# Samples' values in four column groups with a fold at the end, and a new order in the loop of a layer-1 attention kernel

## The reference, cut to what matters

```python
def _nsa_block(qg, gates, q_pos, cmp_k, cmp_v, ksb, vsb, kw, vw, kw_pos):
    s = jnp.einsum('bqghd,bngd->bghqn', qg, cmp_k).astype(jnp.float32) * scale
    p = jax.nn.softmax(jnp.where(cmask, s, NEG_INF), axis=-1) * cmask
    o_cmp = jnp.einsum('bghqn,bngd->bqghd', p.astype(cmp_v.dtype), cmp_v)
    ...
    ps = jax.nn.softmax(jnp.where(smask, ss, NEG_INF), axis=-1)
    o_sel = jnp.einsum('bghqk,bgqkd->bqghd', ps.astype(vsel.dtype), vsel)
    ...
    pw = jax.nn.softmax(jnp.where(wmask, sw, NEG_INF), axis=-1)
    o_win = jnp.einsum('bghqk,bkgd->bqghd', pw.astype(vw.dtype), vw)
    return gates[..., 0:1] * o_cmp + gates[..., 1:2] * o_sel + gates[..., 2:3] * o_win
```

## Time and profile before

| | us |
|---|---|
| median of 3 runs | 977.55 (976.17 to 978.6) |
| the profiled execution | 977.28 |
| its span, first to last instruction | 975.6 |
| attention loop with the samples' keys, window looked at | 684 to 800 |
| the samples' softmax | 800 to 836 |
| the samples' values | 836 to 912 |
| output projection | 912.38 to the end |

### The profile page before, as it was taken

One profiled execution on the slowest core, in us unless ns is written; L12 is line 12 of the kernel. 1 busy time (PEld: TensorE's weight loads), 2 busy tenths in 40 slices (PEclk: granted clock), 3 DMA queues, 4 the chain that ended last, 5 costly groups with the idle time before them and its releaser, 6 DMA issues.

```text
span 975.6 us, 15843 instructions
## 1 busy us (share of the span) xinstructions
PE 921.6 (94%) x5202; PEld 497.5 (51%) x5202; DVE 475.1 (49%) x965; ACT 293.3 (30%) x716; POOL 232.2 (24%) x321
## 2 busy tenths in 40 slices
PE   6999999999899999999999999998888888899998
PEld 3544444444455543454565766566444444556444
DVE  1157778779345552122234172715667776556211
ACT  5101111103454550032101111425555565445100
POOL 0000223210033330430424242001334443234000
PEclk9999999999999999999999999998999998999999
DMA  9142665593254567772414232020211231131211
GB/s 352 57 167 101 226 233 177 193 287 80 45 155 148 156 220 256 220 179 92 143 34 144 73 99 84 16 80 12 65 50 54 74 103 69 48 92 57 89 44 44
DMA packets 86070, 117.59 MB, mean 121 GB/s; under 512 B 21006, under 2 KB 49886, under 8 KB 85678
## 3 DMA queue, kind: packets, MB, share of 16 engines
q1 hardware_dynamic: 66432, 80.96, 25.7%
q0 software_dynamic: 9920, 27.31, 9.5%
q10 hardware_dynamic: 9648, 8.41, 2.7%
HBM read 108.68 MB, written 11.36 MB: 123 GB/s over the span
## 4 chain that ended last, share of the span: by engine, by line
PE 87%; DVE 5%; DMA 3%; ACT 3%; issue 1%; SPq 1%; ACTq 0%; DVEq 0%
PE ps L719 26%; PE ps L976 11%; PE ps L982 6%; PE ps L1269 6%; PE ps L999 4%; PE ps L728 3%; PE ps L1150 3%; PE ps L1161 3%; PE ps L1038 3%; PE ps L914 3%; PE ps L1226 2%; DMA arena<-cache_sb_v 2%; PE ps L892 2%; PE ps L864 1%; PE ps L1016 1%
## 5 line engine op out<-in xcount | busy, mean ns | idle before, releaser
L719 PE MATMUL ps<-wring,arena 128*128 128x512 f32 x448 | 198.4, 602 | 1.5 <-issue 1.5
L719 PEld LDWEIGHTS ps<-wring,arena 128*128 128x128 f32 x448 | 85.2, 192 | 105.8 <-issue 105.7
L667 POOL TENSOR_TENSOR z<-z,work 128x1024 f32<-128x1024 f32 (+1 forms) x64 | 80.2, 1253 | 200.5 <-DVE work L1983 199.7
L976 PE MATMUL ps<-wring,z 128*128 128x512 f32 (+2 forms) x320 | 108.4, 494 | 0.0
L1501 ACT ACTIVATE z<-ps,work 128x512 f32<-128x512 f32 (+3 forms) x128 | 66.6, 527 | 70.3 <-DVE work L1975 58.4
L1324 ACT ACTIVATE z<-ps 128x512 f32<-128x512 f32 (+1 forms) x64 | 27.4, 433 | 181.8 <-PE ps L719 147.5
L976 PEld LDWEIGHTS ps<-wring,z 128*128 128x128 f32 x320 | 55.4, 192 | 44.5 <-issue 42.9
L358 POOL DMA_DIRECT2D arena<-cache_sb_k x64 | 34.4, 537 | 167.4 <-DVE work L1618 143.1
L1823 DVE TENSOR_TENSOR arena<-ps,consts 128x512 f32<-128x512 f32 x32 | 30.4, 1024 | 83.9 <-PE ps L1016 83.9
L1512 ACT ACTIVATE arena<-ps 128x512 f32<-128x512 f32 (+3 forms) x128 | 48.9, 438 | 31.6 <-PE ps L1150 31.6
L1975 DVE TENSOR_REDUCE work<-ps 128x1 f32<-128x512 f32 (+3 forms) x128 | 56.9, 486 | 2.2
(11 more groups left out here) (317 smaller groups left out, 1271.0 us busy)
## 6 DMA issues: line engine op xcount, KB each, us to landing
wring<-w_in SPq DMA_DIRECT2D x12, 2048.0 KB, 9.7
arena<-cache_sb_k POOLq DMA_DIRECT2D x64, 256.0 KB, 3.0
arena<-cache_sb_v SPq DMA_DIRECT2D x64, 256.0 KB, 3.5
wring<-w_out SPq DMA_DIRECT2D x3, 2048.0 KB, 7.8
arena<-cache_sel_k SPq DMA_DIRECT2D x64, 64.0 KB, 1.8
consts<-cache_sel_v SPq DMA_DIRECT2D x64, 64.0 KB, 1.8
consts<-aux SPq DMA_DIRECT2D x1, 2299.5 KB, 16.3
xres<-x_prompt SPq DMA_DIRECT2D x4, 512.0 KB, 10.2
```

The lines of the kernel that those rows point to most:

```text
L667: nc.gpsimd.tensor_tensor(P_u(n), P_u(n), bc(coef(n).unsqueeze(2), [P, 2, (NT - n % NT) * P]), ALU.mult).then_inc(n_scaled, 1)
L719: mm = pe.matmul(ps[:, t, 0:width], stat, mov, start=(k == 0), stop=(k == KT - 1))
L976: mm = pe.matmul(ps[:, bank, at:at + w], normed1(k, t), wring[:, slot, k, lo:lo + w], start=(k == 0), stop=(k == KT - 1))
```

## The change

It has three parts. (1) A sample's 12 products go to four column groups, product m of each page group to output partitions 32m to 32m + 31. DVE masks and sums all 128 partitions into `o_acc`, which takes the place of P's buffer, and at the end four products with a constant 0/1 matrix (`sample_fold`) add the four groups up, one column group for each pair of samples; the sum of branches reads the result in PSUM. (2) On PE the compressed scores and their turn come right behind `scores`, ACT copies the turn before P, and DVE copies keys before `mix` and the compressed weights and takes the compressed maximum earlier. (3) The samples' softmax comes two steps later, and `VALUE_STEPS` and `PTURN_STEPS` with it.

```diff
--- before.py
+++ after.py
...
-       ("forced", NSB), ("block_no", NSB), ("own_sample", 2), ("cmp_neg", NT * NPB), ("cmp_one", NT * NPB),
+       ("forced", NSB), ("block_no", NSB), ("own_sample", 2), ("fold", 2 * HN), ("cmp_neg", NT * NPB), ("cmp_one", NT * NPB),
...
+    put("fold", i[:, None] % (2 * HN) == np.arange(2 * HN)[None, :])
...
-        o_s = work[:, 528:784]
+        o_acc = z[:, NT, P_OFF:P_OFF + NPG * P].rearrange("p (j c) -> p j c", j=NB // 2)
...
-            VALUE_STEPS = {45: 0, 47: 1, 49: 2, 51: 3, 53: 4, 55: 5, 58: 6, 61: 7}
-            PTURN_STEPS = {41: 0, 42: 1, 43: 2}
+            VALUE_STEPS = {47: 0, 49: 1, 51: 2, 53: 3, 55: 4, 57: 5, 59: 6, 61: 7}
+            PTURN_STEPS = {43: 0, 44: 1, 45: 2}
...
-                            mm = pe.matmul(ps[rows_b, 7, (q // 2) * P:(q // 2 + 1) * P], PT1[:, n * P + rows_b.start:n * P + rows_b.stop],
-                                           vsets[b % 2][q][:, m * P:(m + 1) * P], start=(n in (0, 8)), stop=(n in (7, 11)))
+                            mm = pe.matmul(ps[32 * m:32 * m + 32, 7, (q // 2) * P:(q // 2 + 1) * P],
+                                           PT1[:, n * P + rows_b.start:n * P + rows_b.stop],
+                                           vsets[b % 2][q][:, m * P:(m + 1) * P], start=(q != 1), stop=(q != 0))
                     mm.then_inc(sv_used, 1)
+
+                def sample_fold():
+
+                    take(7, *marks_dve.at("sv_sum"))
+                    for j in range(NB // 2):
+                        mm = pe.matmul(ps[32 * j:32 * j + 32, 7, 0:2 * P], cst("fold"), o_acc[:, j], start=True, stop=True)
+                    mm.then_inc(*marks_pe.next("sv_fold"))
...
                         scores(n + 2)
+                    if j == 0:
+                        cmp_scores(i)
+                    if j == 4:
+                        turn_cmp(i)
...
-                    if n == 35:
+                    if n == 37:
                         sample_mask()
...
-                    if j == 0:
-                        cmp_scores(i)
...
-                    if j == 4:
-                        turn_cmp(i)
                 turn_p(NUNIT - 1)
-                for n in range(NUNIT - 3, NUNIT):
+                values(NUNIT - 3)
+                sample_fold()
+                for n in range(NUNIT - 2, NUNIT):
                     values(n)
...
-                    if n >= 1:
-                        copy_p(n - 1)
                     if j == 4:
                         act.wait_ge(nc_turned, i + 1)
                         nc.scalar.activation(p_cmpT, ps[:, 7, :], ACT.Copy).then_inc(nc_T, 1)
+                    if n >= 1:
+                        copy_p(n - 1)
...
-                    if n == 39:
+                    if n == 41:
                         act.wait_ge(*marks_dve.at("sk_max"))
...
-                    rows_b = slice(32 * (b // 2), 32 * (b // 2) + 32)
                     dve.wait_ge(sv_used, b + 1)
-                    mine = cst("own_sample")[rows_b, b % 2:b % 2 + 1]
+                    mine, acc = cst("own_sample")[:, b % 2:b % 2 + 1], o_acc[:, b // 2]
                     if b % 2 == 0:
-                        TS(o_s[rows_b], ps[rows_b, 7, 0:2 * P], mine, None, ALU.mult).then_inc(sv_T, 1)
+                        TS(acc, ps[:, 7, 0:2 * P], mine, None, ALU.mult).then_inc(sv_T, 1)
                     else:
-                        STT(o_s[rows_b], ps[rows_b, 7, 0:2 * P], mine, o_s[rows_b], ALU.mult, ALU.add).then_inc(sv_T, 1)
+                        dve.wait_ge(sv_T, b)
+                        STT(acc, ps[:, 7, 0:2 * P], mine, acc, ALU.mult, ALU.add).then_inc(sv_T, 1)
...
+                    if j == 0:
+                        cmp_max(i)
+                    if i < 4:
+                        for b, q in KEY_STEPS.get(j, [])[0:1]:
+                            sample_keys(2 * i + b, q)
                     if j == 2 and i:
                         mix(i - 1)
                     if j == 2:
                         cmp_weights(i)
-                    if i < 4:
-                        for b, q in KEY_STEPS.get(j, [])[0:1]:
-                            sample_keys(2 * i + b, q)
-                    if n in (36, 37, 38):
-                        sample_softmax(n - 36)
+                    if n in (38, 39, 40):
+                        sample_softmax(n - 38)
...
-                    if j == 0:
-                        cmp_max(i)
...
-                dve.wait_ge(sv_T, NB)
+                dve.wait_ge(*marks_pe.at("sv_fold"))
                 for w in range(2):
                     st.done(TT(o3[:, (w + 1) * P:(w + 2) * P].rearrange("p (g e) -> p g e", g=G),
-                               o_s[:, w * P:(w + 1) * P].rearrange("p (g e) -> p g e", g=G), own, ALU.mult))
+                               ps[:, 7, w * P:(w + 1) * P].rearrange("p (g e) -> p g e", g=G), own, ALU.mult))
```

More of the change, by code:

```diff
@@ L300, in build @@
         marks_dve = Marks(sem("sample_dve"), ["r_dup", "r_kn", "i_max", "i_p", "i_neg", "i_out", "sk_max", "sv_sum", "sv_done"])
-        marks_pe = Marks(sem("sample_pe"), ["r_turned", "r_spread", "i_s", "i_sum", "i_o"])
+        marks_pe = Marks(sem("sample_pe"), ["r_turned", "r_spread", "i_s", "i_sum", "i_o", "sv_fold"])
         marks_act = Marks(sem("sample_act"), ["r_QT", "i_exp", "i_T", "sk_exp"])
```

## The result

The changed kernel takes 969.39 us (median of 4 runs, 968.55 to 970.61); the kernel before, in the same comparison, 978.08 (976.17 to 980.36). The ratio is 0.9921, interval 0.9901 to 0.9941: faster by 0.8%. The prediction was 969.5. The profiled execution of the changed kernel took 969.1 (span 967.4).

The account below looks back on a forecast made before the run. PE was busy 94%, with SP's page issue already at the samples' pace and taking over after the change. Projection at 893.2 + 11.4 = 904.6, 7.8 earlier: 977.28 - 7.8 = 969.5 us; 8-in-10 range 964.5 to 974.5.

Parts of the forecast that it names:

- rival 3: SP's page row does not bind and PE's pace holds: 22 us earlier, 955 us; chance 0.05.
- (a): Key stage: DVE's earlier key copy shortens PE's waits by 1.23 in periods 1 to 3, 0.73 in period 0: 4.4 us.
- (b): Key stage: ACT copies turned compressed scores before P, so keys' turns start 0.31 us earlier in four periods: 1.2 us.
- (c): Softmax and everything behind it two steps later: sample 0 starts at 836.9 us, ends of range 834.7 to 837.7.
- (d): Samples' values in four overlapping column groups: 0.85 us a sample instead of 2.80; DVE's masked sums add nothing.
- rivals 1 and 2: Rival 1: groups don't overlap, 2.80 a sample, 972.7 us, chance 0.10; 2: weight loads exposed, 5.3, 990.1 us, chance 0.05.
- (e): After sample 0, SP's 53.0 us page row takes over: 14 us of new waits, sample 7 at 893.2, 7.0 earlier.
- (f): From sample 7's start to the output projection: 11.4 us instead of 12.17, including 0.5 for the fold.
- The clock's term: Within the end part behind sample 7: PE perhaps at 1.2 GHz after a page wait, 0.7 us taken between 0 and 1.3.
- The sum: Output projection starts at 904.6 instead of 912.38, 7.8 us earlier, giving 969.5 us.
- Rival 4: Moved orders bring nothing because another wait stands behind: 2.2 us earlier, 975.1 us; chance 0.10.

Follow-up runs that it names:

- e1: The changed kernel with SP reading the 48 page numbers of samples 2 to 7 into registers ahead, while idle: 954.15 us, ratio 0.9752.
- e2: The kernel before with SP reading the 48 page numbers into registers ahead, while idle: 976.15 us, ratio 0.9991.
- e6: The kernel before with only the moved orders added: 972.51 us, ratio 0.9962.
- e5: The kernel before with only the four column groups, 128-partition masked sums and fold added: 968.19 us, ratio 0.9923.
- e3: The changed kernel with softmax, turns of P and values back at their old steps: 964.20 us, ratio 0.9870.
- e9: The kernel before with the four column groups and page numbers read ahead, orders and steps as before: 961.32 us, ratio 0.9850.
- e10: The changed kernel without the moved orders, keeping column groups and moved steps: 973.69 us, ratio 0.9966.
- e8: The changed kernel without the moved steps and with page numbers read ahead: 957.27 us, ratio 0.9796.
- e4: The changed kernel with one column group instead of four and no fold, keeping moved orders and steps: 973.13 us, ratio 0.9951.
- e7: The changed kernel with twelve unread filler products before the page waits of samples 3, 5 and 7: 970.45 us, ratio 0.9932.

## Why the prediction was right, point by point

**What bounds.** That SP's row of pages would take over was right and is shown by e1 and e2. It decided the number: without it the time is 954.15, and rival 3 had worked out 955.

**(a)** Right. The copy's 1.23 came out of the wait in full: 1.56 to 0.32, and in period 0 from 2.20 to 1.48, 0.72 where 0.73 was said. PE's timeline of the kernel before, period 0:

```profile
687.60 0.66 PE L989 MATMUL ps<-consts,z 128*128 128x128 f32 x4 [2.20 <-DVE wring L2007]
```

**(b)** Right in size. The wait fell by 0.50, not 0.31 (1.21 to 0.71), but PE reached it later: from the turn of the queries to that of the keys, period 1 takes 719.41 - 712.65 = 6.76 in e6 and 720.91 - 713.82 = 7.09 in e5, 0.33 less. Together (a) and (b) bring 5.75 us by period 3's keys (e6 against e5), where 5.6 was said and the waits alone fell by 6.4.

**(c)** Sample 0's start was to be 836.9. In the changed kernel it is 834.77, which is 169.0 after the loop's first scores; 836.9 would be 168.9 after those of the kernel before. Right in the number, but not in its parts, and that is luck. The two turns of P were to wait 2.2 together behind ACT's copies; they waited 3.06 and 1.64, 4.7 together, and took 1.09 each, against 0.66 in e3. In exchange two waits of the old softmax steps that the sum did not touch, 1.87 and 1.57 for DVE, are gone. PE's timelines, of before and then of after:

```profile
804.91 0.63 PE L1179 MATMUL ps<-consts,wring 128*128 128x128 f32 x4 [1.87 <-DVE wring L2024]
...
828.22 0.66 PE L989 MATMUL ps<-consts,z 128*128 128x128 f32 x4 [1.57 <-DVE wring L2037]
```

```profile
817.72 1.09 PE L1215 MATMUL ps<-consts,z 128*128 128x128 f32 x4 [3.06 <-ACT wring L1504]
...
824.32 1.09 PE L1215 MATMUL ps<-consts,z 128*128 128x128 f32 x4 [1.64 <-ACT wring L1545]
```

And the step gave only where sample 0 comes out; it never priced the move by itself. The starts of sample 0 after the first scores, one execution each, do. With the old orders it is 168.9 to 169.0 in the old steps (before, e2, e5, e9) and 174.1 in the new ones (e10); with the new orders 162.4, 165.3 and 165.5 in the old steps (e3, e6, e8) and 167.4, 169.0, 170.5 and 170.6 in the new ones (e4, the changed kernel, e1, e7). Either way the move costs about 5 us there (by the means with the new orders 169.4 against 164.4), and where SP's row binds behind the groups, it costs them at the end (e3).

**(d)** Right: 0.86 where 0.85 was said, which rules out rivals 1 and 2. The 24 passes alternate between four column groups with new weights each, all in the same rows, in 0.86 us. The rule of the Trainium skill, "TensorE: Matmul & The Clock Gate", part 3, that weight loads overlap only across row groups, does not agree with this row. The masked sums on DVE cost nothing, as said: 128 partitions by 256 columns took 0.48, against 0.47 for 32 partitions:

```profile
836.57 0.48 DVE L2061 TENSOR_SCALAR z<-ps,consts 128x256 f32<-128x256 f32 x1
```

**(e)** Right in kind and size: row 52.84 (53.0 said), 13.4 us of waits before samples 3, 5, 6 and 7 (14 said, over samples 3 to 7; sample 4 had none), sample 7 at 890.90, 225.1 after the first scores (893.2 - 668.02 = 225.2 said).

**(f)** Mis-sized. From sample 7 to the projection it took 904.17 - 890.90 = 13.27, not 11.4. At full clock it is 10.95, in e3, e5, e7, e8 and e9 alike, where the terms without the clock made 10.7. The clock's term was 0.7 and measured 13.27 - 10.95 = 2.3: after the wait of 4.37 not only sample 7's group ran at 1.2 GHz but everything from 889 to 896, at 0.51 on average.

**The sum.** The loop gained 6.0 us in the profiled pair where the sum had 7.8; the error is that of (f). The profiled executions differ by 977.28 - 969.1 = 8.2, because the loop also started 2.3 earlier, most of it by the clock at 440 to 460 us, which no step of the prediction holds and no part of the change explains. The medians differ by 8.7; the ratio's interval is 5.8 to 9.7 us. So the hit to 0.1 us is partly luck: by the loop alone I would have got 971.3, inside the range as well. The chances named for a faster kernel add up to 0.88, not 0.87, which changes nothing.

**What was wrong: the split.** "Of the 7.8, 5.6 come from the moved orders", and about 2 from the column groups. Taken away from the whole, each part agrees with that roughly: without the groups 3.7 are lost (e4), without the orders 4.3 (e10), and by the loops 1.0 and 6.3. But this holds only beside the moved steps, which cost about 5. Alone the groups bring 8.4 and the orders 4.1, and both without the move 13.3. The prediction's own sum held this: its (c) puts sample 0 at 836.9, where it stood in the kernel before (836.88), so that the orders' 5.6 and the two steps cancel and all 7.8 come behind sample 0's start, from the groups. Where a queue's row sets the end, what comes ahead of its start counts in full, as a gain or as a loss; what PE saves behind it counts only up to the queue's pace. The split had the gains and missed the loss. Rival 4 falls with e6, where the orders bring 4.1 by themselves.

## What to carry to other kernels

Where a queue's row of transfers runs without a gap at the pace of its consumer, a faster consumer gains only until the row binds. From then on the end is the row's start plus its length plus what follows its last page, so price every other edit by what it does to the row's start, and look for what can be taken out of the row. Here that was reading the page numbers ahead: 954.15 us, better than both kernels, from an edit that had measured as nothing in the kernel before.

## What the runs showed of the hardware that I had not expected

- A page of 64 KB costs SP 1.10 us to issue, of which only 0.33 is the DMA instruction. With its number already in a register it is 0.52 (e1). The Trainium skill, "DMA: Bandwidth & Descriptors", on issuing engines, calls the time to start a DMA usually small beside the DMA; here it was 1.10 beside 1.84 to land, it set the end, and e1 took 15 us off by it.
- Waits for pages cost twice. After 4.37 us the clock stood at half over 889 to 896 (0.51), and the end part took 2.3 us more; after 1.06 (e5) and 1.40 (e3) at the same place the clock stayed at 1.00 (the end part 10.95). The changed kernel's four runs have mean clocks of 0.977 to 0.982, those of e5 0.979 to 0.988.
- The fold, four products of 256 columns into four column groups, took 0.64 where half of L1199's 1.06 gave 0.5.
